# One stop for the scores of a head: all four row tiles in five PSUM banks, with the products with V and the turns spread behind the quarters of the weight matmuls

## What is computed

```python
h = rmsnorm(x, g_mix); proj = h @ w_in            # q, k, v, u, gate_a, gate_s
# diff_attention: 8 heads, two maps (m = 0, 1) of 64 channels each, v of 128
s = einsum('bhmqd,bhmkd->bhmqk', q_blk, k) * scale
s = s + bias[None, :, None]                       # T5 buckets, one row of bias per head
s = where(rel >= 0, s, -inf)                      # causal
p = softmax(s)
w = p[:, :, 0] - lam * p[:, :, 1]
o = rmsnorm(einsum('bhqk,bhkv->bhqv', w, v), subln_g) * (1 - lam_init)
y = s5_ssm(u, ...)                                # groups of 16 channels, 64 states
z = gelu(y) @ w_glu; ssm = z_val * sigmoid(z_gate)
mixed = sigmoid(gate_a) * o + sigmoid(gate_s) * ssm
x = x + mixed @ w_out
x = x + square(relu(rmsnorm(x, g_mlp) @ w1)) @ w2
out = rmsnorm(x, g_final)
```

## Time and profile before

| | |
|---|---|
| median of three runs | 764.02 us |
| profiled execution | 763.78 us |
| its span, first to last instruction | 762.0 us |
| granted TensorE clock over the span | 0.997 of full speed |
| TensorE matmuls busy | 745.2 us, 98% |
| VectorE busy | 530.5 us, 70% |
| ScalarE busy | 359.2 us, 47% |
| share of the last-ending chain on TensorE | 90% |
| scores (L1922) | from 150.1 to 292.5 us, 128 records |

### The profile page before, as it was taken

One profiled execution on the slowest core, in us unless ns is written; L12 is line 12 of the kernel. 1 busy time (PEld: TensorE's weight loads), 2 busy tenths in 40 slices (PEclk: granted clock), 3 DMA queues, 4 the chain that ended last, 5 costly groups with the idle time before them and its releaser, 6 DMA issues.

```text
span 762.0 us, 10030 instructions
## 1 busy us (share of the span) xinstructions
PE 745.2 (98%) x3754; PEld 608.7 (80%) x3754; DVE 530.5 (70%) x953; ACT 359.2 (47%) x630; POOL 28.3 (4%) x27
## 2 busy tenths in 40 slices
PE   5999999999999999999999999999999999999996
PEld 4878888777777777888888888788888888888885
DVE  4679999665556673436743578866886498748897
ACT  7524631265556663732322645434543345335455
POOL 3210000000000100000000000000000000000015
PEclk9999999999999999999999999999999999999998
DMA  7773439932224430237237130282108320742002
GB/s 246 203 163 116 103 110 163 209 93 71 70 70 122 155 111 3 87 106 248 83 111 194 57 109 29 65 225 98 56 1 235 124 84 0 186 146 83 28 1 111
DMA packets 91824, 85.21 MB, mean 112 GB/s; under 512 B 10028, under 2 KB 68064, under 8 KB 91776
## 3 DMA queue, kind: packets, MB, share of 16 engines
q1 hardware_dynamic: 90944, 82.85, 39.0%
q10 hardware_dynamic: 832, 1.71, 1.1%
HBM read 77.11 MB, written 5.34 MB: 108 GB/s over the span
## 4 chain that ended last, share of the span: by engine, by line
PE 90%; DVE 4%; ACT 3%; issue 2%; DMA 1%; POOL 0%; SPq 0%; DVEq 0%; ACTq 0%
PE ps L1651 27%; PE ps L1653 26%; PE ps L1652 26%; PE ps L1941 3%; PE ps L1922 2%; PE ps L1931 1%; DMA mixA<-in_x 1%; DVE w_lo L1414 1%; PE ps L1726 1%; DVE fr L1427 1%; ACT fa_hi L884 1%; PE ps L1855 1%; ACT w_hi L615 1%; PE ps L1838 1%; PE ps L1815 0%
## 5 line engine op out<-in xcount | busy, mean ns | idle before, releaser
L1651 PE MATMUL ps<-hT_hi,w_hi 128*128 128x512 f32 x384 | 152.5, 397 | 0.5 <-DVE hT_lo L983 0.3
L1653 PE MATMUL ps<-hT_hi,w_lo 128*128 128x512 f32 x384 | 149.9, 390 | 0.0
L1652 PE MATMUL ps<-hT_lo,w_hi 128*128 128x512 f32 x384 | 149.6, 390 | 0.0
L1651 PE MATMUL ps<-w_hi,hT_hi 128*128 128x512 f32 x288 | 113.9, 395 | 1.1 <-POOL w_lo L557 1.1
L1653 PE MATMUL ps<-w_hi,hT_lo 128*128 128x512 f32 x288 | 112.3, 390 | 0.0
L1652 PE MATMUL ps<-w_lo,hT_hi 128*128 128x512 f32 x288 | 112.1, 389 | 0.0
L851 ACT ACTIVATE w_hi<-raw 128x1024 fp32r<-128x1024 f32 x78 | 81.7, 1053 | 56.4 <-PE ps L1653 56.4
L1414 DVE TENSOR_TENSOR w_lo<-raw,w_hi 128x1024 fp32r<-128x1024 f32 x78 | 94.1, 1219 | 16.0 <-ACT w_hi L851 15.0
L615 ACT ACTIVATE w_hi<-raw 128x1024 fp32r<-128x1024 f32 x62 | 64.7, 1057 | 56.7 <-PE ps L1653 51.0
L1011 DVE TENSOR_TENSOR w_lo<-raw,w_hi 128x1024 fp32r<-128x1024 f32 x58 | 70.0, 1220 | 29.5 <-ACT w_hi L615 28.9
L1651 PE MATMUL ps<-w_hi,fa_hi 128*128 128x512 f32 x224 | 87.4, 390 | 1.0 <-DVE w_lo L1414 1.0
(11 more groups left out here) (258 smaller groups left out, 998.0 us busy)
## 6 DMA issues: line engine op xcount, KB each, us to landing
raw<-in_w SPq DMA_DIRECT2D x64, 512.0 KB, 4.2
raw<-in_w_in SPq DMA_DIRECT2D x44, 512.0 KB, 5.3
raw<-in_w_glu SPq DMA_DIRECT2D x8, 512.0 KB, 3.9
raw<-in_w_out SPq DMA_DIRECT2D x8, 512.0 KB, 3.9
mixA<-in_x SPq DMA_DIRECT2D x4, 512.0 KB, 5.1
bias<-frow_dram SPq DMA_DIRECT2D x32, 64.0 KB, 2.0
toep<-taps_dram SPq DMA_DIRECT2D x8, 256.0 KB, 12.5
x<-in_x SPq DMA_DIRECT2D x4, 512.0 KB, 6.7
```

Source lines behind the costliest of these rows:

```text
L1651: nc.tensor.matmul(dst, a_hi, b_hi, start=start, stop=False)
L1652: nc.tensor.matmul(dst, a_hi, b_lo, start=False, stop=False)
L1653: return nc.tensor.matmul(dst, a_lo, b_hi, start=False, stop=stop)
```

## The change

All eight score matmuls of a head now stand together in TensorE's list, at the head's start. Row tile 0 uses banks 0 and 1, tile 1 both halves of bank 5, tile 2 the rest of banks 0 and 1, tile 3 banks 6 and 7. They are issued in the order of `SCORE_ORDER`, so that the two maps of tile 1, which share a bank, don't follow each other, and the second waits for the first (`first_map`). Bank 7 is also that of the readouts. So the 512-column scores wait for `copy_y`, which moves to the front of ScalarE's list for the head, and the readouts wait until VectorE has read the head's scores.

The product with V of block n - 1 now stands between the quarter of weight matmuls of block n and the turn of block n. The product of a head's last block stays behind the next head's scores. The gate tiles of the last head use banks 4 and 5 in place of 4 and 7, and the waits of `turn_y` follow that.

```diff
+    SCORE_ORDER = ((1, 0), (2, 1), (2, 0), (1, 1), (0, 0), (0, 1), (3, 0), (3, 1))
+    def score_place(n, m):
+        i = n % TOK
+        bank, c0 = ((B_SCORE + m, 0), (5, 256 * m), (B_SCORE + m, P), (6 + m, 0))[i]
+        return ps[:, bank, c0:c0 + P * (i + 1)]
+    def scores_needed(n):
+        return TOK * (n // TOK) + (3, 1, 3, 4)[n % TOK]
     def gate_bank(c, t):
-        return (B_QK, B_Y)[t % 2] if c == 4 else t
+        return (B_QK, B_GATE)[t % 2] if c == 4 else t
...
         for a in range(0, BLOCKS, 2):
             h, i = a // TOK, a % TOK
+            if i == 0 and 1 <= h <= UT:
+                copy_y(h - 1)
             exps(a)
...
-            if i == 0 and 1 <= h <= UT:
-                copy_y(h - 1)
...
-            dve.wait_ge(score_ready, n + 1)
+            dve.wait_ge(score_ready, scores_needed(n))
...
-            if b:
-                pe.wait_ge(y_copied, b)
+            pe.wait_ge(score_read, 2 * TOK * (b + 1))
...
-        def scores(n):
+        def scores(h):
             pe.wait_ge(qk_copied, 2 * h + 2)
-            if n < 2:
+            if h == 0:
                 pe.wait_ge(nat_copied, 4 * TOK)
             else:
-                pe.wait_ge(score_read, 2 * n - 2)
-            for m in range(2):
+                pe.wait_ge(score_read, 2 * TOK * h)
+            for i, m in SCORE_ORDER:
+                L = P * (i + 1)
+                if (i, m) == (1, 1):
+                    pe.wait_ge(first_map, h + 1)
+                if (i, m) == (TOK - 1, 0) and 1 <= h <= UT:
+                    pe.wait_ge(y_copied, h)
                 rows = slice(HEAD_DIM * m, HEAD_DIM * m + HEAD_DIM)
-                mm = nc.tensor.matmul(ps[:, score_bank(n, m), 0:L], qT[rows, h % 2, P * i:P * i + P],
+                mm = nc.tensor.matmul(score_place(TOK * h + i, m), qT[rows, h % 2, P * i:P * i + P],
                                       kT[rows, h % 2, 0:L], start=True, stop=True)
-            mm.then_inc(score_ready, 1)
+                if (i, m) == (1, 0):
+                    mm.then_inc(first_map, 1)
+                elif m == 1 and i != 2:
+                    mm.then_inc(score_ready, 2 if i == 0 else 1)
...
-        for a in range(0, BLOCKS, 2):
-            h, i = a // TOK, a % TOK
-            if a and i == 0:
-                pv(a - 2)
...
+        for n in range(BLOCKS):
+            h, i = n // TOK, n % TOK
+            if n == 0:
                 qk_part(2, range(0, 2))
-            scores(a)
-            scores(a + 1)
...
+            if i == 0:
+                scores(h)
+                if h:
+                    pv(n - 1)
+            if h == N_HEADS - 1:
+                gate_tile(i)
+            else:
+                ks = range(4 * (i % 2), 4 * (i % 2) + 4) if n > 1 else (range(2, 6), range(6, 8))[n]
+                qk_part(2 * (h + 1) + i // 2, ks)
+            if i:
+                pv(n - 1)
+            turn_w(n)
+            if i == TOK - 1 and h < UT:
+                readouts(h)
+        row_unit_mm(U_GS + 4, 5, 0, 4, hT_hi, hT_lo, None, 0, range(0, 1))
+        pv(BLOCKS - 1)
+        row_unit_mm(U_GS + 4, 5, 0, 4, hT_hi, hT_lo, None, 0, range(1, 2))
```

More of the change, by code:

```diff
@@ L65 @@
 COL_Q, COL_K, COL_V, COL_U, COL_GA, COL_GS = 0, 1024, 2048, 3072, 3584, 4608
-B_SCORE, B_WT, B_O, B_QK, B_Y, B_S, B_T = 0, 2, 3, 4, 7, 4, 4
+B_SCORE, B_WT, B_O, B_QK, B_GATE, B_Y, B_S, B_T = 0, 2, 3, 4, 5, 7, 4, 4
 def bucket_onehot():
@@ L245, in build @@
     qk_copied = sem("qk_copied")
-    score_ready = sem("score_ready"); score_read = sem("score_read"); nmax_ready = sem("nmax_ready")
+    score_ready = sem("score_ready"); first_map = sem("first_map"); score_read = sem("score_read"); nmax_ready = sem("nmax_ready")
     exp_done = sem("exp_done"); att_step = sem("att_step"); wT_ready = sem("wT_ready")
@@ L357, in qk_bank @@
         return B_SCORE if v == 1 else B_QK
-    def score_bank(n, m):
-        return (B_SCORE, 5)[n % 2] + m
+    SCORE_ORDER = ((1, 0), (2, 1), (2, 0), (1, 1), (0, 0), (0, 1), (3, 0), (3, 1))
[5 more added lines that the diff above has]
+        return TOK * (n // TOK) + (3, 1, 3, 4)[n % TOK]
     def gate_bank(c, t):
-        return (B_QK, B_Y)[t % 2] if c == 4 else t
+        return (B_QK, B_GATE)[t % 2] if c == 4 else t
     def ut_bank(n):
@@ L1299, in pre @@
                 nc.vector.tensor_tensor_reduce(
-                    out=Pm[:, n % 2, m, 0:L], in0=ps[:, score_bank(n, m), 0:L],
+                    out=Pm[:, n % 2, m, 0:L], in0=score_place(n, m),
                     in1=bias[:, h % 2, SEQ - L:SEQ], scale=1.0, scalar=-3e38,
@@ L1697, in nat_free @@
                 elif t == 1:
-                    pe.wait_ge(y_copied, UT)
+                    pe.wait_ge(score_read, 2 * (BLOCKS - 2))
                 else:
@@ L1866, in turn_y @@
             for k in range(UT):
-                if turn_y_bank(k) in (B_QK, B_Y):
+                if turn_y_bank(k) in (B_QK, B_GATE):
                     pe.wait_ge(nat_copied, 5 * TOK)
@@ L1910, in _ @@
             qk_part(v, range(KT))
-        def scores(n):
-            h, i = n // TOK, n % TOK
-            L = P * (i + 1)
+        def scores(h):
             pe.wait_ge(qk_copied, 2 * h + 2)
-            if n < 2:
+            if h == 0:
                 pe.wait_ge(nat_copied, 4 * TOK)
             else:
-                pe.wait_ge(score_read, 2 * n - 2)
-            for m in range(2):
+                pe.wait_ge(score_read, 2 * TOK * h)
[5 more added lines that the diff above has]
+                    pe.wait_ge(y_copied, h)
                 rows = slice(HEAD_DIM * m, HEAD_DIM * m + HEAD_DIM)
-                mm = nc.tensor.matmul(ps[:, score_bank(n, m), 0:L], qT[rows, h % 2, P * i:P * i + P],
+                mm = nc.tensor.matmul(score_place(TOK * h + i, m), qT[rows, h % 2, P * i:P * i + P],
                                       kT[rows, h % 2, 0:L], start=True, stop=True)
-            mm.then_inc(score_ready, 1)
+                if (i, m) == (1, 0):
+                    mm.then_inc(first_map, 1)
+                elif m == 1 and i != 2:
+                    mm.then_inc(score_ready, 2 if i == 0 else 1)
         def turn_w(n):
@@ L1959, in gate_tile @@
                 mm.then_inc(nat_ready, 1)
-        for a in range(0, BLOCKS, 2):
-            h, i = a // TOK, a % TOK
-            if a and i == 0:
-                pv(a - 2)
-            if a == 0:
-                qk_part(2, range(0, 2))
-            scores(a)
-            scores(a + 1)
[L1969 to L1979, removed]
+        for n in range(BLOCKS):
+            h, i = n // TOK, n % TOK
+            if n == 0:
+                qk_part(2, range(0, 2))
+            if i == 0:
[11 more added lines that the diff above has]
+            if i == TOK - 1 and h < UT:
                 readouts(h)
-        for j in range(2):
-            row_unit_mm(U_GS + 4, 5, 0, 4, hT_hi, hT_lo, None, 0, range(j, j + 1))
-            pv(BLOCKS - 2 + j)
+        row_unit_mm(U_GS + 4, 5, 0, 4, hT_hi, hT_lo, None, 0, range(0, 1))
+        pv(BLOCKS - 1)
+        row_unit_mm(U_GS + 4, 5, 0, 4, hT_hi, hT_lo, None, 0, range(1, 2))
         turn_y()
```

## The result

The changed kernel takes 765.50 us in the median of 22 runs, against 764.07 us for 22 runs of the kernel before on the same chip. The ratio is 1.0019, 95% interval 1.0011 to 1.0027. So it is slower by 1.4 us, and the forecast was 765.3. Its profiled execution took 765.45 us, with a span of 763.7 us and a granted clock of 0.999. In the page, the busy time of TensorE falls, its share falls too, and the chain that ends last holds less of TensorE (83%, before 90%) and more of VectorE and ScalarE.

A forecast was written before the change was run, and what follows sets the result against it. TensorE, busy 98% of the span, was taken as the bound; its saving would turn into waits for VectorE. Head 0 +0.29, heads 1-3 3*0.18, heads 4-6 3*0.38, head 7 -0.51: +1.5, so 765.3 us, range 763.0 to 766.7.

The forecast's parts named there:

- TensorE's saving: Second score visit and readout tile changes go: 0.39 us a head, 0.20 more in four; TensorE alone gains 3.9 us.
- Head 7: Last head, twice the weight matmuls, so nothing is late: -0.51 us.
- the two waits for ScalarE: TensorE's waits in heads 0 and 7, 0.40 and 0.22 us, would both go.
- Rival C: First V product's wait is small, TensorE keeps its gain: 760.3 us if whole, 762 if half; chance 0.12.
- Late start of VectorE: First bias-add of a head starts at S+1.72 us (S: start of its scores), not S+0.54.
- Wait at the first V product: Heads 1 to 6: TensorE waits 0.4 to 0.6 us for VectorE's gating, until 9.72 us after the scores' start.
- Head 0: First head, scores to next scores: 17.83 us, before 17.54; about 1.2 us of wait before the third turn.
- No ACT wait: Expected sign in the new profile: TensorE no longer waits for ScalarE anywhere.
- Third turn: Third turn of the weights in a head: TensorE there at S+13.41 us, VectorE's input allowing it at S+13.36.
- just in time: At the third turn, VectorE's weights of row tile 2 release TensorE at 13.36 us, TensorE arriving at 13.41.
- rival B: Unequal score pairs run in step or wait for each other: +0.9 us, 766.2 us; chance 0.18.
- The sum: All heads: +0.29 (head 0), 3*0.18 (heads 1-3), 3*0.38 (heads 4-6), -0.51 (head 7): +1.5 us.

The follow-up runs named there:

- e7: Changed kernel with VectorE's gating ahead of its split, k halves of `qk_part` in bank 5, and head 0's second split behind row tile 3: 760.11 us.
- e8: Kernel before with three spare VectorE operations ahead of each head's first bias-add: 765.32 us.
- e1: Changed kernel with VectorE's gating of the head before moved ahead of its split of weights: 764.64 us.
- e4: Kernel before with only the V products spread behind the quarters of weight matmuls, scores still in two visits: 769.69 us.
- e5: Changed kernel with VectorE's gating ahead of its split and the k halves of `qk_part` in bank 5: 761.37 us.
- e10: Changed kernel with the first V product of a head behind the second turn instead of ahead of it: 764.49 us.
- e6: Changed kernel with only the k halves of `qk_part` moved to bank 5, VectorE's list as it was: 765.55 us.
- e2: Kernel before with VectorE's gating moved ahead of its split of weights: 764.40 us.

## Why the prediction was right

**TensorE's saving: right in size.** Scores of a head 2.46 us (forecast 1.50 more than 0.86, and 0.10). From the last readout row to the scores 0.32 us (206.81 to 207.13), of which the row's four records take 0.22; the other 0.10 is ahead of the change, and another 0.10 lies in the first passes of the scores: 0.20 for the change, as taken. Head 7, where nothing is late, went from 31.99 to 31.42 us between its scores and `turn_y`: -0.57, forecast -0.51. The whole of the saving shows in e7: -4.0 us, where the prediction had -3.7 (3.9 and 0.6 for the two waits for ScalarE, less 0.8 for `first_map`). Rival C had its price right (760.3), and its condition wrong for this kernel: the wait at the first V product had to go, and two things more.

**Late start of VectorE: right.** S+1.71, forecast S+1.72. It has two consequences, told apart by e8 and e1: 1.17 us of delay are more than the slack of 0.92 (a delay of 0.86, in e8, was not), and the gating comes too late for a V product that comes earlier.

**Wait at the first V product: right.** S+9.71, forecast S+9.72; waits of 0.5 us in heads 1 to 6, put down to the gating; periods 19.62 and 17.71, forecast 19.59 and 17.70. e4, e5 and e10 each vary this wait alone or with its twin, and the time follows.

**Head 0: right in sum, not in its parts.** 17.84, forecast 17.83. One wait of 1.2 us was forecast at the third turn. There are two, 0.34 for the copy of q and 0.38 at the turn; without the first the turn alone waits 0.98 (e6). "No ACT wait" was thus wrong. The same omission made e1 miss: what was hidden behind the expected wait had not been listed.

**Third turn: the time right, the limit not.** The release was put at 0.14 from one row; at this turn it is 0.07 (e10). VectorE would allow S+13.26, so "just in time" was a margin of 0.15 us a head, and e10 picks it up: its third turn comes 0.15 earlier.

**Head 5: not foreseen, +0.45 us.** 18.16 and not 17.71. VectorE beside GpSimd's copy of y there:

```profile
255.52 2.29 POOL L576 COPY y_rows<-y_nat 128x512 f32<-128x512 f32 x4 [204.53 <-DMA y_nat<-y_dram]
...
256.49 0.22 DVE L1312 TENSOR_SCALAR nmx<-mx 128x2 f32<-128x2 f32 x1
...
256.81 0.45 DVE L1319 SCALAR_TENSOR_TENSOR cfac<-rinv,sums,nlam 128x1 f32<-128x1 f32 x1
257.29 0.92 DVE L1322 SCALAR_TENSOR_TENSOR Pm<-Pm,cfac 128x384 f32<-128x384 f32 x1
...
258.27 0.55 PE L1944 MATMUL ps<-ident,Pm 128*128 128x128 f32 x3 [0.23 <-DVE Pm L1322]
```

The same operations take 0.17, 0.22 and 0.62 us in the other heads. They grow by 0.05, 0.23 and 0.30, 0.58 together; less the margin of 0.15, that is nearly the 0.45. The copy is four instructions of 0.62 us each. This is the third alone:

```profile
256.63 0.61 POOL L576 COPY y_rows<-y_nat 128x512 f32<-128x512 f32 x1
```

It ends at 257.25, and the operation of 256.81 at 257.26. In the kernel before the copy lies over an earlier part of the head, where one operation was stretched, and the slack took it:

```profile
253.69 1.18 POOL L568 COPY y_rows<-y_nat 128x512 f32<-128x512 f32 x2
...
254.52 0.37 DVE L1304 TENSOR_SCALAR nmx<-mx 128x2 f32<-128x2 f32 x1
...
255.25 0.62 DVE L1314 SCALAR_TENSOR_TENSOR Pm<-Pm,cfac 128x384 f32<-128x384 f32 x1
```

The operation of 254.52 ends at 254.89, and the last copy at 254.87.

The Trainium skill (SBUF — State Buffer, SBUF: two separate sides) says that a VectorE operation with two inputs in SBUF, or in a two-port mode, and a GpSimd operation exclude each other for a whole instruction, and the later one blocks. The traces agree: in nine traces an operation on one or two columns is stretched by 0.05 us or more beside the copies, fourteen times in all, and each time it ends 8 to 24 ns behind the end of one of the four copies. The 384-column one is met by a copy in five traces, and ends 0.41 us behind that copy's end each time. The bias-adds, which read PSUM, keep their 0.69 us beside the copies.

No run moved the copy on purpose, but it starts at another place in each. e6 has the changed kernel's VectorE list and the same periods. There the copy begins at S+9.46 and not S+11.08, and ends at 257.28, ahead of the three operations (here the second):

```profile
254.98 2.30 POOL L576 COPY y_rows<-y_nat 128x512 f32<-128x512 f32 x4 [204.03 <-DMA y_nat<-y_dram]
...
257.84 0.22 DVE L1319 SCALAR_TENSOR_TENSOR cfac<-rinv,sums,nlam 128x1 f32<-128x1 f32 x1
```

Head 5 of e6 takes 17.70 us, with no extra, and the 384-column operation 0.62. In e1 and e4, with the copy at S+8.56 and S+9.68, there is no extra either; in e2, e5, e7, e8 and e10, with the copy at S+10.44 to S+10.99, there is one of 0.23 to 0.65 us.

**The unequal pairs (rival B): they don't run in step.** In the single records of TensorE's scores in head 3, the passes of the lower row tile start at 0, 320, 536 and 859 ns (256, then 384 columns), and those of the upper at 7, 434, 756 and 1074 ns (384, then 256 columns). Each keeps its own pace, 0.22 us a pass of 256 columns and 0.32 of 384, but for the first passes, which take 0.10 more in both (the fill). The 0.10 us for `first_map` lies between the two passes of the 256-column score that waits, which are 318 ns apart and not 218. So rival B is out, and the 0.10 that the prediction took for `first_map` was right.

**The sum.** To the start of head 7 the heads gave +0.30, +0.22, +0.22, +0.19, +0.39, +0.84 and +0.41, and head 7 -0.57: +2.0. The spans differ by 1.7 (763.7 and 762.0), the medians by 1.4. Forecast was +1.5, without head 5's 0.45. What takes back 0.3 us (0.07 ahead of head 0, 0.22 behind the start of `turn_y`) is not settled; it is of the size in which two executions differ. Head by head, but for head 5, the forecast is right to 0.1 us in all. That the total is as close is in part luck, since head 5's 0.45 and these 0.3 nearly cancel.

## What to carry to other kernels

On an engine that is 98% busy, work moved forward also takes away the cover of every wait that it had hidden: list for each buffer who empties it and when, not only the wait that will be the longest. Waits that lie one upon the other have no prices of their own; here the removal of one was worth 0.9 us (with the accident of head 5 in it), of the other nothing, and of both 4.1. Before a group of matmuls is gathered to save their starts, ask how much later its first result comes for the next engine, and how much slack that engine has: here 1.17 us later against 0.92 us.

## What the runs showed of the hardware

- Two float32 matmuls of unequal size on the two 64-row halves of the array run independently: starts 7 ns apart, then each at its own pace.
- To change from 128*64 to 64*128 tiles costs 0.20 us, like each way from and to 128*128: 0.10 ahead of the first matmul and 0.10 in its first pass. The matmul that waits for `first_map` starts in time and still loses 0.10 us before its second pass.
- From the end of VectorE's last operation to TensorE's matmul it takes 0.07 us (third turn) to 0.14 us (first V product).
- TensorE loses more by a wait than the idle time that the profile lists: 0.71 us at the third turn for 0.50 at the V product (changed kernel against e5).
- A small VectorE operation on SBUF that meets a GpSimd copy of 128x512 float32 from SBUF to SBUF (0.62 us) ends 8 to 24 ns behind the end of that copy (kernel before, changed, e2 to e5, e7, e8, e10), and so grows by 0.05 to 0.39 us. A bias-add from PSUM keeps its length.
